# Sample projection in two 64-column halves of TensorE, later q/k transposes, chunk 1's K copies ahead of its weights

## What is computed

```
hn = rmsnorm(x, g_mix);  p = hn @ w_in            # 1024 -> 3072 columns: q | k | v | B | C | xv
q, k, v: 8 heads of 64;  u = C * xv
prompt: stick-breaking attention over the 512 tokens
sample: stick-breaking attention over the 8 new tokens and 4096 cached ones
        (32 pages of 128 tokens per sequence, found by page_table, newest page first)
h = x + concat(rmsnorm(attn), rmsnorm(B * conv3(u))) @ w_out
h = h + cross_attention(rmsnorm(h));  h = h + swiglu(rmsnorm(h));  y = rmsnorm(h)
also returned: k and v rows, conv state, memory k and v
```

## Time and profile before

| | us |
|---|---|
| median of 3 runs (lowest, highest) | 1221.96 (1218.54, 1224.35) |
| the profiled execution | 1218.36 |
| its span, from first to last instruction | 1216.7 |
| PE / DVE / ACT / POOL busy | 1118.7 / 626.5 / 396.9 / 407.8 |
| mean granted TensorE clock | 0.977 |

### The profile page before, as it was taken

The page is one execution under the profiler, slowest core; times in us unless marked ns, Lnnn a source line. Parts: engine busy times, 40 slices in busy tenths (PEclk is TensorE's granted clock), DMA queues, the critical chain, the costliest instruction groups (busy, mean ns, idle before and its releaser), DMA issues.

```text
span 1216.7 us, 25953 instructions
## 1 busy us (share of the span) xinstructions
PE 1118.7 (92%) x9815; PEld 981.3 (81%) x9815; DVE 626.5 (51%) x853; ACT 396.9 (33%) x624; POOL 407.8 (34%) x341
## 2 busy tenths in 40 slices
PE   6889999989877999799799888899999999999997
PEld 2678888867655777567599867899999999999996
DVE  1645533554644777576389456745553002554544
ACT  2633232233443656464433253421211111212111
POOL 0324435323322343244433103343343433433330
PEclk9999999989988999999999999899999999999999
DMA  9657767657898899998862042322212223221222
GB/s 358 216 166 248 272 241 278 239 181 258 302 333 281 293 348 317 308 328 292 288 242 66 6 139 74 101 70 86 86 61 77 79 95 104 69 90 56 65 65 78
DMA packets 126409, 220.69 MB, mean 181 GB/s; under 512 B 9935, under 2 KB 68564, under 8 KB 126308
## 3 DMA queue, kind: packets, MB, share of 16 engines
q1 hardware_dynamic: 103154, 146.37, 35.2%
q0 software_dynamic: 20480, 67.13, 16.1%
q10 hardware_dynamic: 2674, 5.87, 1.4%
HBM read 213.52 MB, written 5.80 MB: 180 GB/s over the span
## 4 chain that ended last, share of the span: by engine, by line
PE 76%; DVE 11%; DMA 5%; ACT 3%; issue 2%; SPq 1%; POOLq 0%; ACTq 0%; POOL 0%; DVEq 0%
PE ps L514 37%; PE ps L1568 14%; PE ps L1649 8%; PE ps L1674 4%; DMA k_page<-in_cache_sb_k 3%; PE ps L1706 3%; PE ps L1513 2%; PE ps L575 2%; DVE r_sq L672 1%; DVE run L1334 1%; DVE r_sum L677 1%; DMA v_late<-in_cache_sb_v 1%; DVE h_lo L419 1%; DVE run_s L1317 1%; PE ps L358 1%
## 5 line engine op out<-in xcount | busy, mean ns | idle before, releaser
L470 POOL TENSOR_TENSOR w_lo<-w_raw,w_hi 128x2048 fp32r<-128x2048 f32 (+3 forms) x49 | 192.9, 3939 | 395.9 <-ACT w_hi L447 359.8
L514 PE MATMUL ps<-h_hi,w_hi 128*128 128x288 f32 x832 | 180.2, 298 | 8.7 <-DVE h_lo L419 5.7
L514 PE MATMUL ps<-h_hi,w_lo 128*128 128x288 f32 x832 | 179.1, 297 | 0.0
L514 PE MATMUL ps<-h_lo,w_hi 128*128 128x288 f32 x832 | 179.1, 297 | 0.0
L1649 PE MATMUL ps<-cc,k_page 128*128 128x128 f32 x1024 | 140.3, 288 | 38.7 <-DVE kT L1307 15.8
L1649 PEld LDWEIGHTS ps<-cc,k_page 128*128 128x128 f32 x1024 | 116.2, 146 | 61.7 <-issue 41.5
L447 ACT ACTIVATE w_hi<-w_raw 128x2048 fp32r<-128x2048 f32 (+3 forms) x47 | 77.8, 1660 | 255.1 <-PE ps L514 227.2
L611 POOL DMA_DIRECT2D v_late<-in_cache_sb_v x168 | 90.3, 537 | 176.7 <-issue 109.0
L514 PEld LDWEIGHTS ps<-h_hi,w_hi 128*128 128x128 f32 x832 | 135.3, 190 | 9.7 <-issue 7.2
L514 PEld LDWEIGHTS ps<-h_hi,w_lo 128*128 128x128 f32 x832 | 135.0, 190 | 0.0
L514 PEld LDWEIGHTS ps<-h_lo,w_hi 128*128 128x128 f32 x832 | 135.0, 190 | 0.0
(11 more groups left out here) (251 smaller groups left out, 1837.6 us busy)
## 6 DMA issues: line engine op xcount, KB each, us to landing
k_page<-in_cache_sb_k SPq DMA_DIRECT2D x256, 256.0 KB, 5.3
v_late<-in_cache_sb_v POOLq DMA_DIRECT2D x168, 256.0 KB, 5.3
v_early<-in_cache_sb_v POOLq DMA_DIRECT2D x88, 256.0 KB, 4.8
mw_raw<-in_w_in SPq DMA_DIRECT2D x12, 1024.0 KB, 5.6
w_raw<-in_w_gate SPq DMA_DIRECT2D x11, 1024.0 KB, 5.3
w_raw<-in_w_up SPq DMA_DIRECT2D x11, 1024.0 KB, 5.3
w_raw<-in_w_down SPq DMA_DIRECT2D x8, 768.0 KB, 4.4
w_raw<-in_w_down SPq DMA_DIRECT2D x8, 640.0 KB, 4.0
```

Source lines behind the costliest of these rows:

```text
L470: return nc.gpsimd.tensor_tensor(w_lo[s][:, ks, :], w_raw[s][:, ks, :], w_hi[s][:, ks, :].bitcast(F32), ALU.subtract)
L514: op = nc.tensor.matmul(ps[:, 2 * t + hf, 0:b - a], weights[s][:, k, t * P:(t + 1) * P], x[:, k0 + k, a:b], start=begin and k == ks[0] and ...
```

## The change

1. The projection of the sample rows (L1513) is cut in two halves of TensorE's columns: q goes to bank 0, partitions 0 to 63, while v goes to bank 0, partitions 64 to 127; the first 256 columns of k go to bank 1, partitions 0 to 63, the last 256 to partitions 64 to 127. Each k-tile is four products (512, 512, 256, 256 columns) instead of three of 512. For this `x_s` is loaded twice, to rows 0-63 and 64-127, and ACT's square, root and DVE's reciprocal run over 128 partitions. The v rows are read from partitions 64 to 127; the k rows come out in two DVE instructions of 256 columns.
2. `bias_col` counts for `masks_and_bias_loaded` and not for the constants; DVE's `bias_dg` and PE's bias products wait for both loads there.
3. ACT does `tile_hi(0)` ahead of all eight `h_hi`. The sample part of `x_rms` goes to bank 3 instead of 7. `tile(0)` comes directly after `x_rms` and waits for neither the root nor the q/k copies. The q and k rows are transposed after it, all in bank 4; DVE copies q, then ACT copies k, then `new_scores` may run. DVE's `queries(0)` and everything behind it wait for the q copy.
4. ACT's `tile_hi(2)` stands right after `copy_k(0)`.
5. DVE's `weights(1, 3, SEQ)` stands in chunk 0 behind `evac(1)` and `copy_k(1)`, instead of ahead of them.

```diff
--- before.py
+++ after.py
@@ -223,8 +223,9 @@
 
         s_id, s_x = sem("identity_loaded"), [sem(f"x_loaded{i}") for i in range(3)]
         s_const, s_m, s_pt = sem("consts_loaded"), sem("mem_loaded"), sem("ptab_loaded")
-        s_set, s_masks = sem("ones_and_token_set"), sem("masks_loaded")
+        s_set, s_masks = sem("ones_and_token_set"), sem("masks_and_bias_loaded")
         s_qkv_a, s_vrow = sem("sample_qkv_first_rows"), sem("sample_v_row")
+        s_qk = sem("sample_q_k_transposed_then_copied")
         s_tr, s_ev = sem("unit_transposed"), [sem("bank4_copied"), sem("bank5_copied")]
         s_bmm, s_bc = sem("bias_product"), sem("bias_copied")
         s_full = [sem("weights_loaded0"), sem("weights_loaded1")]
@@ -300,8 +301,6 @@
                        ([st_rows[0:2 * BS, j * P:(j + 1) * P] for j in range(4)], stT[:, :, :])])
         U_X = batch([([x_tok[:, m, (4 * kh + j) * P:(4 * kh + j + 1) * P] for j in range(4)],
                       xT[:, 4 * kh:4 * kh + 4, m * P:(m + 1) * P]) for m in range(NB) for kh in range(2)])
-        U_QK = batch([([r[0:NS, j * P:(j + 1) * P] for j in range(4)], pT[:, t:t + 4, SEQ:T])
-                      for r, t in ((q_rows, T_Q), (ks_rows, T_K))])
 
         I_V = [([vT[:, j, m * P:(m + 1) * P] for m in range(NB)], v_tok[:, 0:NB, j * P:(j + 1) * P]) for j in range(HP)]
         I_K = [([pT[:, T_K + j, m * P:(m + 1) * P] for m in range(NB)], k_rows[:, :, j * P:(j + 1) * P]) for j in range(HP)]
@@ -873,7 +872,8 @@
         @block.sync
         def _(sp):
             sp.dma_start(cc[:, 0:P], shape_consts[:, 0:P]).then_inc(s_id, 16)
-            sp.dma_start(x_tok[0:NS, NB, :], x_s.rearrange("b t n -> (b t) n")).then_inc(s_x[2], 16)
+            for half in range(2):
+                sp.dma_start(x_tok[half * NS:(half + 1) * NS, NB, :], x_s.rearrange("b t n -> (b t) n")).then_inc(s_x[2], 16)
 
             def sample_weights(i):
                 k0, k1, _ = WS_PLACE[i]
@@ -974,17 +974,16 @@
             act.dma_start(vec_rows[G_FIN:G_FIN + 8, :], g_fin.rearrange("(k p) -> k p", p=P)).then_inc(s_const, 16)
             act.dma_start(vec_rows[W_CONV:NVEC, :], w_conv[0].rearrange("j (k p) -> (j k) p", p=P)).then_inc(s_const, 16)
             act.dma_start(st_rows[0:2 * BS, :], st_conv[0].rearrange("b k n -> (b k) n")).then_inc(s_const, 16)
-            act.dma_start(bias_col[0:HEADS, :], sb_bias[0].rearrange("(h o) -> h o", o=1)).then_inc(s_const, 16)
+            act.dma_start(bias_col[0:HEADS, :], sb_bias[0].rearrange("(h o) -> h o", o=1)).then_inc(s_masks, 16)
             act.wait_ge(s_set, 2)
 
             def square(m):
-                r = rows_of(m)
                 if m < NB:
                     act.wait_ge(s_x[m // 2], 16)
                     act.wait_ge(s_sq["inb"], m + 1)
                 else:
-                    act.wait_ge(s_x[2], 16)
-                nc.scalar.activation(x_sq[0:r, :], x_tok[0:r, m, :], ACT.Square, accum_out=x_ss[0:r, m:m + 1])\
+                    act.wait_ge(s_x[2], 32)
+                nc.scalar.activation(x_sq[:, :], x_tok[:, m, :], ACT.Square, accum_out=x_ss[:, m:m + 1])\
                     .then_inc(s_sq["inb"], 1)
 
             tr_copy(act, even(U_XS))
@@ -992,7 +991,7 @@
             square(NB)
             nc.scalar.preload_act_table(ACT.Sqrt)
             act.wait_ge(s_sq["inb"], 1)
-            nc.scalar.activation(x_ss[0:NS, 7:8], x_ss[0:NS, NB:NB + 1], ACT.Sqrt, bias=cst[0:NS, 0:1], scale=1.0 / D)\
+            nc.scalar.activation(x_ss[:, 7:8], x_ss[:, NB:NB + 1], ACT.Sqrt, bias=cst[:, 0:1], scale=1.0 / D)\
                 .then_inc(s_rs, 1)
             for m in range(NB):
                 square(m)
@@ -1145,19 +1144,19 @@
                         .then_inc(s_sq_early, 1)
 
             copied(act, U_X[-1])
-            hi_parts(act, "inb", xT, G_MIX, range(4))
             tile_hi(0)
-            hi_parts(act, "inb", xT, G_MIX, range(4, KD))
+            hi_parts(act, "inb", xT, G_MIX, range(KD))
             act.wait_ge(s_ms["inb"], 1)
             nc.scalar.activation(rstd[:, 0:SEQ], ps[:, 6, 0:SEQ], ACT.Sqrt, bias=cst[:, 0:1], scale=1.0 / D)
-            nc.scalar.activation(rstd[:, SEQ:T], ps[:, 7, 0:NS], ACT.Sqrt, bias=cst[:, 0:1], scale=1.0 / D)\
+            nc.scalar.activation(rstd[:, SEQ:T], ps[:, 3, 0:NS], ACT.Sqrt, bias=cst[:, 0:1], scale=1.0 / D)\
                 .then_inc(s_rt["inb"], 1)
             act.wait_ge(s_rs, 2)
             act.wait_ge(s_qkv, 1)
             copied(act, U_VEC[-1])
-            nc.scalar.activation(v_tok[0:NS, NB, :], ps[0:NS, 2, :], ACT.Copy, scale=x_ss[0:NS, 7:8]).then_inc(s_vrow, 1)
-            tr_copy(act, even(U_QK))
+            nc.scalar.activation(v_tok[0:NS, NB, :], ps[NS:P, 0, :], ACT.Copy, scale=x_ss[NS:P, 7:8]).then_inc(s_vrow, 1)
             tile_hi(1)
+            act.wait_ge(s_qk, 2)
+            nc.scalar.activation(pT[:, T_K:T_K + 4, SEQ:T], tiled(ps[:, 4, 256:512], NS), ACT.Copy).then_inc(s_qk, 1)
             act.wait_ge(s_vrow, 1)
             act.wait_ge(s_qrows, 1)
             for src, dst in ((v_tok[0:NS, NB, :], out_v_s), (ks_rows[0:NS, :], out_k_s)):
@@ -1168,6 +1167,7 @@
                 nc.scalar.activation(x_sq[:, :], m_tok[:, m, :], ACT.Square,
                                      accum_out=x_ss[:, 5 + m:6 + m]).then_inc(s_sq["ck"], 1)
             copy_k(0)
+            tile_hi(2)
             act.wait_ge(s_ms["ck"], 1)
             nc.scalar.activation(rstd_m[:, :], ps[:, 6, 0:NMEM], ACT.Sqrt, bias=cst[:, 0:1], scale=1.0 / D)\
                 .then_inc(s_rt["ck"], 1)
@@ -1176,7 +1176,6 @@
             sample_sigmoids(0, NS)
             copy_weights(0, True)
             sample_sigmoids(1, SEQ)
-            tile_hi(2)
             for g in range(GROUPS):
                 group(g, g == GROUPS - 1)
 
@@ -1247,10 +1246,11 @@
             copied(dve, U_VEC[-1])
             gain = cvec[:, G_MIX:G_MIX + KD].rearrange("p (k o) -> p k o", o=1).to_broadcast([P, KD, NS])
             nc.vector.tensor_tensor(xg_s[:, :, :], xT[:, :, SEQ:T], gain, ALU.mult).then_inc(s_set, 1)
+            dve.wait_ge(s_masks, 32)
             nc.vector.tensor_scalar(bias_dg[0:HEADS, :], ident[0:HEADS, 0:HEADS], bias_col[0:HEADS, 0:1], None,
                                     ALU.mult).then_inc(s_set, 1)
             dve.wait_ge(s_rs, 1)
-            nc.vector.reciprocal(x_ss[0:NS, 7:8], x_ss[0:NS, 7:8]).then_inc(s_rs, 1)
+            nc.vector.reciprocal(x_ss[:, 7:8], x_ss[:, 7:8]).then_inc(s_rs, 1)
             step(dve, nc.vector.memset(q_bd[:, :, :, :], 0.0))
             def convolve(k):
                 w = [cvec[:, W_CONV + 4 * j + k:W_CONV + 4 * j + k + 1] for j in range(3)]
@@ -1377,6 +1377,8 @@
                         evac(2 * C + 1)
                     if C + 1 < CHUNKS:
                         copy_k(C + 1)
+                    if C == 0:
+                        weights(1, 3, SEQ)
                     if c == 7 and not last:
                         queries(g + 1)
                     if 2 * C + 2 < TILES:
@@ -1431,11 +1433,13 @@
             lo_parts(dve, "inb", xT, G_MIX, range(4))
             dve.wait_ge(s_rs, 2)
             dve.wait_ge(s_qkv, 1)
-            nc.vector.tensor_scalar(ks_rows[0:NS, :], ps[0:NS, 1, :], x_ss[0:NS, 7:8], None, ALU.mult)
+            nc.vector.tensor_scalar(ks_rows[0:NS, 0:256], ps[0:NS, 1, 0:256], x_ss[0:NS, 7:8], None, ALU.mult)
+            nc.vector.tensor_scalar(ks_rows[0:NS, 256:512], ps[NS:P, 1, 0:256], x_ss[NS:P, 7:8], None, ALU.mult)
             nc.vector.tensor_scalar(q_rows[0:NS, :], ps[0:NS, 0, :], x_ss[0:NS, 7:8], None, ALU.mult).then_inc(s_qrows, 1)
             lo_parts(dve, "inb", xT, G_MIX, range(4, KD), 0, 4)
-            tr_copy(dve, odd(U_QK))
-            copied(dve, U_QK[-1])
+            dve.wait_ge(s_qk, 1)
+            nc.vector.tensor_copy(pT[:, T_Q:T_Q + 4, SEQ:T], tiled(ps[:, 4, 0:256], NS)).then_inc(s_qk, 1)
+            dve.wait_ge(s_qk, 2)
             queries(0)
             rms_inv(dve, "inb", rstd[:, :])
             for m in range(MT):
@@ -1446,7 +1450,6 @@
             copy_k(0)
             weights(0, 0, NS)
             rms_inv(dve, "ck", rstd_m[:, :])
-            weights(1, 3, SEQ)
             for g in range(GROUPS):
                 group(g, g == GROUPS - 1)
 
@@ -1501,21 +1504,21 @@
         @block.tensor
         def _(pe):
             pe.wait_ge(s_id, 16)
-            pe.wait_ge(s_x[2], 16)
+            pe.wait_ge(s_x[2], 32)
             tr_pe(pe, U_XS)
-            pe.wait_ge(s_const, 16 * 10)
+            pe.wait_ge(s_const, 16 * 9)
             tr_pe(pe, U_VEC)
             pe.wait_ge(s_set, 3)
             for i, (k0, k1, _) in enumerate(WS_PLACE):
                 pe.wait_ge(s_wsl[i], 16)
                 for k in range(k0, k1):
-                    for n in range(3):
-                        op = nc.tensor.matmul(ps[0:NS, n, :], xg_s[:, k, :], w_s[i][:, k - k0, n * CH:(n + 1) * CH],
-                                              start=k == 0, stop=k == KD - 1)
```

(20 more changed lines are left out.)

## The result

The changed kernel takes 1210.49 us in the median of 5 runs (1204.37 to 1211.49), the kernel before 1221.96 (1218.54 to 1224.35): a ratio of 0.990, 95% interval 0.9871 to 0.9928. The forecast was 1209.9. The profiled execution took 1204.37 with a span of 1202.7; it is the fastest of its five, so its distance to the profiled execution of before (14.0 us) is larger than that of the medians (11.5).

The account below looks back on a forecast made before the run. TensorE, 76% of the page's chain, was taken as the bound, so its start-up idle counted. Gains of 8.0 (tile(1)) - 1.3 (half clock) + 5.4 (chunk 1) = 12.1 us off 1221.96 gave 1209.9 us, range 1203.5 to 1218.

Parts of the forecast that it names:

- 8.0 - 1.3: Start-up up to tile(1): 8.0 us gained from the earlier first K copy, less 1.3 us for a half clock.
- lower bound: Total: smallest gain, 5.0 us, with slower queries, longer half clock, dearer k rows and tile_hi(2); time 1217 us.
- queries and half clock: Ahead of and around tile(1): queries(0) taken at 1.0 us, bound 2.4; half clock at 1.3, bound 3.4.
- Projection: Start-up projection: halves run side by side, 1.31 us per k-tile for 2.63, ending at 31.2 instead of 41.9.
- no overlap: Projection rival: halves don't run side by side, projection ends at 41.5; gain 4.4 us, 1217.6 us; chance 0.05.
- a slow clock at the start: Start of the projection: a slow clock makes the first 30 passes cost 2.3 us more.
- The slack of the rows on VectorE: Chunk 0: DVE reaches the k and q rows 3.7 us after the projection's end, which no longer ends the wait.
- tile(0) and what is behind it: Chunk 0: tile(0) ends at 40.2 instead of 55.1; first K copy at 47.8 instead of 56.07, 8.3 us earlier.
- Clock: K transposes and tile(1): one half-clock stretch behind TensorE's new idle costs 1.3 us, between 0 and 3.4.
- The rival of the lasting low clock: Last K transposes and all of tile(1): clock stays low; gain 6.0 us, 1216 us; chance 0.09.
- Chunk 1: Between tile(1) and tile(2): with weights(1) behind the K copies, pages end at 73.8 against 79.2, gaining 5.4 us.
- Given back in the chunks: From 300 us on: bandwidth-limited K-page stream turns the earlier start into waits; 12.1 to 0 left, 1220 us; chance 0.10.

Follow-up runs that it names:

- e3: Changed kernel with the projection again as three products of 512 columns in partitions 0 to 63; 1221.24 us in a single run, against 1222.96 before.
- e2: Kernel before with only weights(1) moved behind evac(1) and copy_k(1); 1217.51 us against 1222.96 before.
- e6: Changed kernel with q/k transposes again ahead of tile(0) and the first four h_hi ahead of tile_hi(0); 1210.51 us against 1223.15 before.
- e4: Changed kernel with the first four h_hi again ahead of tile_hi(0) on ScalarE; 1211.64 us against 1222.96 before.
- e8: Changed kernel with root and reciprocal per token ahead of x_rms and ScalarE's m_tok squares ahead of its k copy; 1207.71 us against 1223.15 before.
- e5: Kernel before with only the projection in two halves, including the second x_s load and 128-partition statistics; 1213.26 us against 1223.15 before.
- e1: Changed kernel with weights(1) put back ahead of evac(1) and copy_k(1) on VectorE; 1217.77 us against 1222.96 before.
- e7: e6 with root and reciprocal taken per token (5 columns) ahead of x_rms; 1201.58 us against 1223.15 before.

## Why the prediction was right, point by point

**Total.** Faster by 11.5 in the medians, 12.1 forecast. But the start-up gives 9.6 and not 12.1: 4.3 at tile(1) where the sum had 6.7 (8.0 - 1.3), and 5.3 behind it (5.4). In part the forecast is right by luck of the rest, which a measurement of this kernel can't resolve. Its own lower bound was added up wrongly: queries and half clock were taken off whole (2.4 and 3.4), though 1.0 and 1.3 of them were in the 12.1 already. Put right, the bound is a gain of 7.4 and not 5.0, a time of 1214.6 and not 1217; the 11.5 lies inside either.

**Projection.** Right: halves side by side, 1.36 us a k-tile for 1.31, end at 32.0 for 31.2. The prediction says that no run so far shows a pair of 64 columns, and overlooks one. The prompt sums of the kernel before (L1634) write their two heads to partitions 0 to 63 and 64 to 127, and from 461.36 us on the second head's passes start beside the last ones of the first (461.360 and 461.366); 16 passes start within 1.31 us, where 0.109 apart, as in one half, they would need 1.64. The case against "no overlap" was thus stronger than rows 4. The 2.3 us put down to a slow clock at the start are read from the pace (passes 0.86 apart until 17, then 0.43); the profile's column of the granted clock shows 1.00 there, so that the clock is the cause is not shown.

The worth of the halves in the whole is 6.5 of 9.6 (e3). The slack of the rows on VectorE, sized at 3.7, was 5.2 (the rows began at 37.2), but it isn't the slack that counts: PE's own in tile(0), 3.2, ends first, and the prediction didn't name it.

**h_lo.** The order was right, a term was missing. mw_raw landed at 30.79 (30.1 forecast), h_lo 7 was done at 41.8 (39.4). DVE's four h_lo were put at 0.75 each, from rows where POOL stood still; here POOL's low part ran beside the first of them, and it took 1.96. The prediction had seen the same thing on queries(0) and did not ask which other DVE instruction would now meet POOL. That is 1.5 of the 2.4; the landing is 0.7. In the eight profiled executions with the second x_s load mw_raw landed between 30.2 and 32.3, in the two without it (before, e2) at 29.5. With the load it comes later in all eight, by 0.7 to 2.8, in the mean 2.1 where 0.65 were taken; no run adds the load alone.

**tile(0) and what is behind it.** End at 43.1 (40.2). 2.4 of the 2.9 are h_lo, 0.5 come from a wrong assumption: tile(0) was to end one k-tile behind h_lo 7, but VectorE makes an h_lo in 0.75 us and PE needs 0.86 for its k-tile, so PE falls behind and ends 1.3 us after h_lo 7, four k-tiles (3.45) after h_lo 4. From there to the first K copy 7.0 (7.6 forecast): queries took 0.78 (1.0 taken, bounds 0.7 and 2.4), since POOL's second low part was over in time, by 0.2 us:

```profile
39.92 4.15 POOL L940 TENSOR_TENSOR mw_lo<-mw_raw,mw_hi 128x1024 fp32r<-128x1024 f32 x1 [5.46 <-ACT mw_hi L1010]
...
44.28 0.78 DVE L1354 COPY q_bd<-pT 64x32 f32<-64x32 f32 x4
```

The first K copy is 5.9 earlier instead of 8.3: 2.9 lost up to tile(0)'s end and 0.6 won behind it. POOL's low part was to end at 41.9 and ended at 44.1 (it took 4.15 and not 2.4, beside h_lo 4 to 7); that queries, later by as much, still escaped it was luck. That the deferral of the q/k transposes itself was a loss was in the sum (15 us at tile(0), 8 kept), but was not said: e6 against e4 shows 4.7 us at tile(1).

**Clock.** Right in kind, nearly in size. Stretches of the changed kernel (us, busy of five engines, granted clock, DMA share, GB/s), as in the earlier trace rows:

```profile
48.00:50.00 2.00, 1.09 (x4) 0.72 (x4) 1.97 (x5) 0.95 (x2) 0.78 (x3) 0.50 1.06 396
50.00:52.00 2.00, 1.03 (x5) 1.06 (x6) 1.39 (x3) 0.00 (x0) 1.02 (x2) 0.50 1.03 408
52.00:54.00 2.00, 2.00 (x12) 2.00 (x11) 0.69 (x1) 0.80 (x2) 0.56 (x2) 0.50 1.03 396
```

The clock is half, 1.2 of 2.4 GHz, from 48 to 54, behind a stretch in which PE was busy for 1.25 of 4 us (44 to 48); it meets the last K pages (3.65 against 2.03 in e8: 1.6 us) and spares tile(1) (6.37). Forecast 1.3. The rival of the lasting low clock is down, but was near: in e5 the half clock falls on tile(0), in e4 in part on tile(1).

**Chunk 1.** 5.3 measured, 5.4 forecast, and independent of the earlier start-up (e1, e2). weights(1) ran from 70.27 to 72.45 under tile(2), as said, and its product took 0.69 and not the 2.7 taken, since POOL's low part was over by then.

**Rest of the kernel.** "Given back in the chunks" is down as far as the medians can tell: the starts of the scores in chunks 1 to 8 are all 9.6 earlier, and the totals of the changed kernel and of e1 to e8 lie between 2.0 below and 3.0 above their start-up gains, 1 above in the mean. The scatter arises between chunk 8 and chunk 31. From the scores of the one to those of the other the ten profiled executions need 349.0 (changed) to 358.5 us (e6), 352.9 before and 355.7 in e7, which is no order by start-up gain; behind them nine of the ten agree within 1.2 us. Which waits in the chunks make up these 9.5 us was not traced.

## What to carry to other kernels

Work taken off the busiest engine is worth only what the next engine in the row leaves of it: follow each engine's queue to the first instruction that the next stage needs, and ask what of it used to run under the work that is now short or moved. Don't move a product ahead of the small steps that it used to hide; here the long reciprocal belonged under tile(0), and better still ahead of the broadcast, where it is 5 columns wide. When a stage starts earlier, list which instruction pairs of VectorE and GpSimd now coincide.

## What the runs showed of the hardware

- Two-input VectorE instructions and short SBUF copies that meet a running GpSimd elementwise instruction wait for its end: h_lo 1.96 us for 0.75, the copies of queries(0) 2.95 for 0.78, while an instruction that reads PSUM is not held: the K copies of chunk 1 in the changed kernel take 0.69 each at 67.72, beside GpSimd's 66.50 to 68.87. Nor is a reciprocal held, though it reads and writes SBUF: in the changed kernel one of 576 columns starts at 603.68, inside a low part of GpSimd (601.59 to 606.19), and takes its 3.75 us. The Trainium skill ("GPSIMD Engine Reference", 1. Specifications) says that GpSimd's SBUF interfaces are shared with VectorE, with contention for instructions with two SBUF inputs or in a 2-port mode; the traces agree with the 1.96, of an instruction with two such inputs; in which mode the copies of the 2.95 ran, no view shows. The wait goes the other way too when VectorE is first: GpSimd's low part, begun at 39.92 among h_lo 4 to 7, took 4.15 us and ended 2.2 behind the last of them; alone it takes 2.36.
- fp32 products in two halves of TensorE's columns run side by side in full: 1.36 us for 8 passes (4 of 512, 4 of 256 columns), against 2.63 for 6 of 512 in one half.
- A half clock (granted clock 0.50) of some 6 us behind an idle of PE costs 1.6 us if it meets short transposes that wait for copies anyway; where it falls on tile(0), in e5, tile(0) takes 8.27 us against 6.39 for tile(1).
